# Two layers of a hybrid diffusion backbone on one core: the borders between blocks worked in two sets of 320 tokens

## The reference

```
h = rmsnorm(x, g[2*s]) * (1 + scale[s]) + shift[s]
y = block_s(h)          # s=0: FFN, s=1: token mixing, s=2: FFN
x = x + (0.5 or 1) * gate[s] * rmsnorm(y, g[2*s+1])
FFN(h) = (silu(h @ w1) * (h @ w3)) @ w2      # 1024 -> 2816 -> 1024
```

## Time and profile before

| | us |
|---|---|
| median of 3 runs | 3273.2 |
| the profiled execution, its own time | 3275.5 |
| its span, first to last instruction | 3273.7 |
| PE busy | 2971.1 (91%) |
| POOL busy | 1361.0 (42%) |
| DVE busy | 972.3 (30%) |
| ACT busy | 580.3 (18%) |
| mean granted PE clock | 0.951 |

### The profile page before, as it was taken

How to read it: one execution, slowest core, us unless ns; L and a number is a source line. 1 busy time by engine, 2 the same in 40 slices (tenths; PEclk the granted TensorE clock), 3 DMA queues, 4 the chain that set the end, 5 groups by cost and what they waited for, 6 DMA issues and landing times.

```text
span 3273.7 us, 50932 instructions
## 1 busy us (share of the span) xinstructions
PE 2971.1 (91%) x21012; PEld 2812.1 (86%) x21012; DVE 972.3 (30%) x1580; ACT 580.3 (18%) x974; POOL 1361.0 (42%) x1556
## 2 busy tenths in 40 slices
PE   6999999898978899999979999997988787999996
PEld 3999999798877799999969999997988776999996
DVE  3110111624546531011141101116245465210112
ACT  2000001312213421000130000013131145110111
POOL 1445445333322335544524454453332223455553
PEclk8999999899888899999989999998998888999998
DMA  6332332211102112233213323322110021112211
GB/s 261 129 124 88 129 128 89 86 67 44 44 26 90 53 42 67 83 129 128 96 65 128 116 96 129 124 92 84 51 52 30 27 91 52 62 62 89 70 64 59
DMA packets 46370, 281.89 MB, mean 86 GB/s; under 512 B 5089, under 2 KB 10721, under 8 KB 20513
## 3 DMA queue, kind: packets, MB, share of 16 engines
q1 hardware_dynamic: 39024, 259.46, 22.2%
q10 hardware_dynamic: 7216, 20.60, 1.7%
HBM read 270.07 MB, written 9.97 MB: 86 GB/s over the span
## 4 chain that ended last, share of the span: by engine, by line
PE 84%; DVE 8%; ACT 3%; issue 2%; DMA 1%; DVEq 1%; POOL 0%; ACTq 0%; SPq 0%
PE ps L527 25%; PE ps L529 24%; PE ps L528 24%; PE ps L559 2%; ACT rstd L964 2%; PE ps L753 1%; PE ps L696 1%; ACT arena L964 1%; DVE rstd L1386 1%; PE ps L716 1%; PE ps L736 1%; DMA first_raw<-in_w_mod 1%; DVE arena L1350 1%; PE ps L548 1%; PE ps L760 1%
## 5 line engine op out<-in xcount | busy, mean ns | idle before, releaser
L477 POOL TENSOR_SCALAR wsplit<-raw 128x512 fp32r<-128x512 f32 (+2 forms) x776 | 443.6, 600 | 1872.3 <-issue 831.2
L527 PE MATMUL ps<-h,wsplit 128*128 128x320 f32 (+1 forms) x3488 | 1106.1, 317 | 76.6 <-DVE rstd L1386 32.4
L528 PE MATMUL ps<-h,wsplit 128*128 128x320 f32 (+1 forms) x3488 | 1086.4, 311 | 0.0
L529 PE MATMUL ps<-h,wsplit 128*128 128x320 f32 (+1 forms) x3488 | 1086.0, 311 | 0.0
L482 POOL TENSOR_TENSOR wsplit<-raw,wsplit 128x512 fp32r<-128x512 f32 (+2 forms) x776 | 924.4, 1224 | 0.0
L527 PEld LDWEIGHTS ps<-h,wsplit 128*128 128x128 f32 (+1 forms) x3488 | 662.1, 190 | 116.2 <-DVE rstd L1386 57.6
L528 PEld LDWEIGHTS ps<-h,wsplit 128*128 128x128 f32 (+1 forms) x3488 | 663.0, 190 | 0.0
L529 PEld LDWEIGHTS ps<-h,wsplit 128*128 128x128 f32 (+1 forms) x3488 | 661.8, 190 | 0.0
L527 PE MATMUL ps<-hidden,wsplit 128*128 128x320 f32 x1408 | 435.8, 310 | 3.6 <-issue 3.6
L529 PE MATMUL ps<-hidden,wsplit 128*128 128x320 f32 x1408 | 435.1, 309 | 0.0
L528 PE MATMUL ps<-hidden,wsplit 128*128 128x320 f32 x1408 | 435.1, 309 | 0.0
(11 more groups left out here) (171 smaller groups left out, 2517.0 us busy)
## 6 DMA issues: line engine op xcount, KB each, us to landing
raw<-in_w SPq DMA_DIRECT2D x88, 1024.0 KB, 6.4
raw<-in_w_mod SPq DMA_DIRECT2D x60, 1024.0 KB, 4.9
raw<-in_w SPq DMA_DIRECT2D x64, 704.0 KB, 4.2
raw<-in_w_in SPq DMA_DIRECT2D x30, 1024.0 KB, 4.9
first_raw<-in_w_mod SPq DMA_DIRECT2D x12, 1024.0 KB, 5.0
raw<-in_w_out SPq DMA_DIRECT2D x8, 768.0 KB, 4.3
spill<-xT ACTq DMA_DIRECT2D x2, 2560.0 KB, 7.6
xT<-spill ACTq DMA_DIRECT2D x2, 2560.0 KB, 13.8
```

The costliest lines, as they stand in the source:

```text
L477: nc.gpsimd.tensor_scalar(w[:, 0, at], src[:, at], 1.0, 1.0, ALU.mult, ALU.mult)\
L527: mm(out, w[0], x[0], start=first, stop=False)
L528: mm(out, w[0], x[1], start=False, stop=False)
L529: return mm(out, w[1], x[0], start=False, stop=last)
```

## The change

- The last two down units of an FFN (units 6 and 7 of the second group) are claimed together and worked as half 0 of both, then half 1 of both; the sum of squares of half 0 is multiplied within half 1 of the first. DVE evacuates them by halves.
- The output projection makes 16 pieces of six matmuls, first half 0 of all 8 tiles, then half 1, in a ring of six PSUM banks.
- All squares, roots, outgoing and incoming norm steps of a border are made for tokens 0 to 319 and then for 320 to 639 (`tokens`, `token_parts`), with DVE's outgoing steps of half 1 placed between its incoming steps of half 0, and ACT's squares likewise.
- The first products of a block (`enter`) run for half 0 as its h comes, with the sums of half 1's squares in between, then for half 1. In border 0 two pieces of the input projection (half 0) stand between the two halves of the gates. In border 1 the first **two** up units are worked together. In border 2 it is the first up unit.
- Counters' initial increments for layer 1 are made at the head of the whole program of PE and DVE.
- The output is two transfers, each when its half of x is there, issued by SP in the main block.
- The four modulation operations for the next borders (`prepare`) stand between the outgoing steps of half 1.

```diff
-for _u, _parts in ((U_C, FEAT), (U_C + 1, FEAT), (U_C + 2, TOK), (U_C + 3, TOK),
+for _u, _parts in ((U_C, FEAT_BY_HALF), (U_C + 1, FEAT), (U_C + 2, TOK), (U_C + 3, TOK),
...
+                for a in range(2):
+                    sp.wait_ge(signals[-1].x_ready, x_count(2, a, KT - 1))
+                    sp.dma_start(O["y"][:, :, tokens(a)], xT[:, :, tokens(a)]).then_inc(y_out, 16)
+                sp.wait_ge(y_out, 32)
...
+                    def border_sums(b, l_in, s):
+                        for k in range(4):
+                            x_sums(l_in, s, 0, k)
+                        y_sums(b, 1)
+                        for k in range(4, KT):
+                            x_sums(l_in, s, 0, k)
+                    def enter(s, units, more=None):
+                        for a in range(2):
+                            pe.wait_ge(sig.rstd_ready, in_count(l, s, a))
                             for k in range(KT):
+                                pe.wait_ge(sig.h_ready, h_count(l, s, a, k))
+                                for base, blocks in units:
+                                    for b, w in enumerate(blocks):
+                                        c = base + (2 * b + a) * BANK
+                                        last = three_pass(ps[0:w.shape[3], c:c + HALF], (w[:, 0, k, :], w[:, 1, k, :]),
+                                                          [h2[:, p, k, tokens(a)] for p in range(2)],
+                                                          k == 0, k == KT - 1)
+                                    if a and k == KT - 1:
+                                        last.then_inc(sig.unit_done, 1)
+                                if a == 0:
+                                    x_sums(l, s, 1, k)
+                            if a == 0 and more:
+                                more()
...
+                            elif mods:
+                                enter(s, [(claim(f), up_weights(f))])
+                                turn()
                             else:
+                                enter(s, [(claim(u), up_weights(u)) for u in (f, f + 1)])
...
+                        bases = [claim(n + KT - 2 + u) for u in range(2)]
+                        for a in range(2):
+                            for u in range(2):
+                                w = split_ap(l, n + KT - 2 + u, GF_T * P).rearrange("p s (f c) -> p s f c", f=GF_T)
+                                c = bases[u] + a * BANK
+                                for k in range(GF_T):
+                                    last = three_pass(ps[:, c:c + HALF], (w[:, 0, k, :], w[:, 1, k, :]),
+                                                      [a2[:, p, k, tokens(a)] for p in range(2)],
+                                                      k == 0, k == GF_T - 1)
+                                    if a and u == 0 and k == 7:
+                                        y_sums(s, 0)
+                                last.then_inc(sig.unit_done if a else half_done, 1)
...
-                        first_products(1, base, (w,))
+                        enter(1, [(base, (w,))], lambda: dense(2))
...
-                    sums(1, U_GATES)
-                    sums(2, U_GATES)
+                    border_sums(0, l, 1)
                     gates()
-                    dense(11)
+                    dense(9)
...
+                    ring = (0, 1, 4, 5, 6, 7)
+                    for a in range(2):
+                        for m in range(KT):
+                            q = a * KT + m
+                            if q >= len(ring):
+                                pe.wait_ge(sig.y_sum, q - len(ring) + 1)
...
+                            if q == KT + 4:
+                                y_sums(1, 0)
+                    border_sums(1, l, 2)
                     ffn(2, 1)
-                    sums(5, U_ALL[l])
+                    if l + 1 < DEPTH:
+                        pe.wait_ge(sig.unit_evac, EV(U_ALL[l] - 1))
+                        mod(U_FFN[0], l=l + 1, sig=signals[l + 1])
+                        border_sums(2, l + 1, 0)
+                    else:
+                        y_sums(2, 1)
...
+                            half_y(0, 0)
+                            add_square(b, KT - 3)
+                            half_y(1, 0)
+                            add_square(b, KT - 2)
+                            add_square(b, KT - 1)
+                            half_y(0, 1)
+                            for k in range(3):
+                                out_step(b, 0, k)
+                            add_square(b, KT)
+                            half_y(1, 1)
+                            for k in range(3, 5):
+                                out_step(b, 0, k)
+                            add_square(b, KT + 1)
+                            for k in range(5, KT + 1):
+                                out_step(b, 0, k)
+                        for k in range(3):
+                            out_step(b, 1, k)
+                        if prepare:
+                            dve.drain()
+                            prepare()
                         for k in range(KT + 1):
+                            if l_in < DEPTH:
+                                in_step(l_in, s, 0, k)
+                            if k + 3 <= KT:
+                                out_step(b, 1, k + 3)
+                        if l_in < DEPTH:
+                            for k in range(KT + 1):
+                                in_step(l_in, s, 1, k)
```

More of the change, by code:

```diff
@@ L88 @@
 FEAT = [("feat", m, a) for m in range(2) for a in range(2)]
+FEAT_BY_HALF = [("feat", m, a) for a in range(2) for m in range(2)]
 TOK = [("tok", 0, 2), ("tok", 2, 2), ("tok", 4, 1)]
@@ L549, in mod_turn, with first_sums @@
                         last.then_inc(sig.mtr_done, 1)
[L551 to L555, removed]
-                            for k in range(KT):
[L557 to L568, removed]
+                    def first_sums():
+                        pe.wait_ge(sig.acc_add, KT)
+                        for a in range(2):
+                            last = mm(ps[:, (2 + a) * BANK:(2 + a) * BANK + HALF], ones, rstd[:, tokens(a)],
+                                      start=True, stop=True)
+                        last.then_inc(sig.ss_done, 1)
@@ new lines, in y_sums, with x_sums @@
+                    def y_sums(b, a):
+                        y = Y_STEPS[b]
+                        pe.wait_ge(sig.acc_add, KT + Y_BASE[b] + y.index((KT - 1, a)) + 1)
+                        mm(ps[:, (2 + a) * BANK:(2 + a) * BANK + HALF], ones, rstd[:, tokens(a)],
+                           start=True, stop=True).then_inc(sig.ss_done, 1)
+                    def x_sums(l, s, a, k):
+                        pe.wait_ge(xsq_ready, xsq_count(l, s, a, k))
+                        last = mm(ps[:, (2 + a) * BANK:(2 + a) * BANK + HALF], ones, yT[:, k, tokens(a)],
+                                  start=k == 0, stop=k == KT - 1)
+                        if k == KT - 1:
+                            last.then_inc(signals[l].ss_done, 1)
@@ new lines, in h_upper, with border @@
+                    def h_upper(l, s, a, k):
+                        act.wait_ge(signals[l].hmul_ready, h_count(l, s, a, k))
+                        for c, cols in token_parts(a):
+                            last = fn(h2[:, 0, k, cols], yT[:, k, cols], ACT.Identity,
+                                      bias=modS[:, 3 * KT * s + k, c:c + 1])
+                        last.then_inc(signals[l].h_hi, 1)
+                    def border(b, l_in, s):
+                        out = lambda a: root(l, rstd_count(l, b, f"out{a}"), a)
+                        last = l_in == DEPTH
+                        if b == 1:
+                            for i in range(KT + 5):
+                                y_step(b, i)
+                            out(0)
+                            for i in range(KT + 5, 2 * KT):
+                                y_step(b, i)
+                        else:
+                            for i in range(KT):
+                                y_step(b, i)
+                                if i == KT - 3:
+                                    ln_exp()
+                            out(0)
+                            y_step(b, KT)
+                            if not last:
+                                x_square(b, 0, 0)
+                                x_square(b, 0, 1)
+                            y_step(b, KT + 1)
+                        if last:
+                            out(1)
+                            return
+                        for k in range(2 if b != 1 else 0, 6):
+                            x_square(b, 0, k)
+                        out(1)
+                        for k in (6, 7):
+                            x_square(b, 0, k)
+                        root(l_in, in_count(l_in, s, 0), 0)
+                        for k in range(KT):
+                            h_upper(l_in, s, 0, k)
+                            x_square(b, 1, k)
```

(3 more changed lines are left out.)

294 lines of the change are left out of this document (163 added, 131 removed).

## The result

The changed kernel takes **3327.0 us** (median of 4 runs, 3326.3 to 3329.4) against 3273.7 for the kernel before beside it; the ratio is 1.0165, 95% interval 1.0153 to 1.0178. Forecast were 3322, and 3293 to 3346 as the range. The profiled execution took 3329.4, with a span of 3327.6 (before 3273.7) at a mean granted clock of 0.950 (before 0.951); it is the slowest of the four.

The account below looks back on a forecast made before the run. TensorE (PE), 84% of the span, was taken as the bound, losing by waits and half clock. Border 0 twice 20.8, border 1 twice 27.0, border 2 1.0 and the end -0.3 gave +48.5 us: 3322, range 3293 to 3346.

Parts of the forecast that it names:

- F: Border 2 between the layers: 45.4 us against 53.3, increments' wait gone, with the paired down units' cost +1.0 us.
- G: Kernel end: 17.7 us behind unit 7, plus 8.9 for the paired down units, against 26.9: -0.3 us.
- A: Last down units at each FFN end, four times: PE waits 6.3 us for unit 7's split, restarts slow: +8.9 us.
- B: Border 0, twice, from unit 7's end to the gates' end: 40.9 us against 41.4, -0.5 us.
- C: Dense pieces between the gate halves, twice: PE stands 7.0 us waiting for ACT, no gain, cold restart: +2.0 us.
- D: Border 1, twice: half-sum delays PE, two up units leave little room, 62.2 us against 59.9: +4.2 us.
- E: Third up unit, twice: two units hold both buffers, PE waits 7.3 us for POOL's split, restarts cold: +9.3 us.
- The contention: Border 0: POOL's split of the first input unit slows twelve DVE operations, +5.7 us, bounds 0 and 7.6.
- the half-sum behind piece 12: Border 1, output projection: PE waits for eight ACT steps; with the sum itself +1.9 us.
- the second transfer: Kernel end: output transfer of 1280 KB, in no row, taken as 5.6 us, between half and all of 7.9.
- The price of a half add: DVE's half adds in the borders: taken as 0.40 us, between 0.37 and 0.48.
- The rival that the overlap wins: Splits in place in time at FFN ends and third up unit: -3 us, 3250 without contention; chance 0.10.

Follow-up runs that it names:

- e4: Changed kernel with both dense pieces of the input projection behind both halves of the gates again: 3320.8 us, ratio 1.0141 to the kernel before.
- e1: Changed kernel with unit 7 claimed only behind half 0 of unit 6: 3297.4 us, ratio 1.0069 to the kernel before.
- e8: Changed kernel with the last two down units in turn, each claimed by itself, half-sum in half 1 of unit 7: 3301.2 us, ratio 1.0084.
- e2: Changed kernel with half 1 of the first two up units in border 1 worked one unit after the other: 3311.3 us, ratio 1.0111.
- e6: Changed kernel with POOL's split of the first input unit cut to 8 columns an instruction, leaving out part of the computation: 3314.8 us, ratio 1.0125.
- e5: Changed kernel with unit 7 claimed late, one up unit entering border 1, and dense pieces behind the gates: 3272.5 us, ratio 0.9994.
- e7: Kernel before with only layer 1's initial increments moved to the head of PE's and DVE's programs: 3265.5 us, ratio 0.9977.

## Why the prediction was right, point by point

Measured in the profiled execution, layer 0 (F and G where they are):

| step | forecast | measured | from |
|---|---|---|---|
| A, x4 | +8.9 | +9.2 | unit 5's end to unit 7's end 28.6 (571.4 to 600.0), before 19.4 |
| B, x2 | -0.5 | +0.3 | unit 7's end to the gates' end 41.7 (to 641.7) for 41.4 |
| C, x2 | +2.0 | +3.0 | 14.5 shift at 1126.82, less A, B and 2.0 at the start; e4: 3.05 |
| D, x2 | +4.2 | +2.3 | second up unit 1205.8 |
| E, x2 | +9.3 | +9.4 | 23.5 from second to third up unit, before 14.1 |
| F | +1.0 | +2.1 | shift from 26.3 to 28.4 |
| G, with its A | -0.3 | +0.2 | 17.7 behind unit 7, before 26.9 |

With A inside F and G, 2 x (9.2 + 0.3 + 3.0) + 2 x (2.3 + 9.4) + 2.1 + 0.2 = 50.7. The spans differ by 53.9. Another 2.0 is there before the first up unit (86.3 for 84.3): the first weights arrive at 19.9 in place of 16.7. That is no effect of the change, as e1 and e8, with the same code there, have them at 17.2 and 17.0. Of the last 1.2 most is in border 1 of layer 1, where the kernel before is 0.9 faster than in layer 0 (89.9 for 90.8): its restart before the output projection costs 1.6 there and 2.5 in layer 0, behind the same wait of 3.9 (last section).

That the sum came so near is in part luck: D was 1.9 too high, twice, while A, B, C and F, all too low, make up for it.

**A and E, the two that decide**, held in cause and size: waits of 6.4 and 7.3 for the 6.3 and 7.3, slow products for 4.4 to 5.4 us for the 4.5 (a choice between bounds, no reading: behind the stop at 1112.30 the kernel before has 5.5), and e1 and e2 took them away by the buffer alone. Together they are 4 x 9.2 + 2 x 9.4 = 55.6 us; all the rest, C included, is -4.9.

**B.** The chain without contention came out as worked (adds 0.40 apart, roots as priced), and so did its end: 41.7 for 40.9. The contention was 6.1 by e6, for 5.7. The Trainium skill's page SBUF — State Buffer (section "SBUF: two separate sides") has a DVE operation with two SBUF inputs and one of POOL take the shared pair for a whole instruction; the 7.6 which that gave is 1.5 too much, and my 5.7 was 0.4 too little. The rows agree with taking turns (POOL's four take 5.91 where nearly alone they take 5.02, and DVE's start as far apart as POOL's), but POOL's 1.3 and DVE's 0.40 would make 1.7 a turn, and it is 1.47, so some of each overlaps.

**C** was undersized by 1.0. The place was right (6.87 of wait on ACT, by its own order of work). The slow stretch behind it lasts from 648.7 to 654.2, 20 products, which costs 2.6 and not 2.0; the last 0.4 isn't traced.

**D** failed in one term: the half-sum behind piece 12 cost 0.85, not 1.9. PE's wait for it was 0.15; the projection starts at the slow clock, which gives the chain of squares time, and that I had left out (argued, not tested). The parts of the rest are off in both directions (last product to half 0's root 19.5 for 21.2, half 0 of both units 21.3 for 20.0) and leave 61.3 for 62.2.

**F**: 46.2 behind unit 7 for 45.4; how much of it the contention makes (8.1 in the forecast) no run separates. **G**: 17.7 for 17.7; the second transfer takes 5.7 from its issue (3321.9) to the end, for the 5.6 taken between the bounds.

**The price of a half add**, 0.40, was what the chains of B, F and G lay on, and it is 0.40 (3312.37, 3312.77 and on, in the end). The Trainium skill's page VectorE: DVE Perf Modes (section "The TRN2 errata") gives 0.49 for it; that is what the trace has as its duration (0.48), while its successor starts 0.40 later. Halving doubles only what doesn't overlap, 0.07 us an add.

**The rival that the overlap wins** was right that the two waits decide between a loss and none: with the splits nearly in place the change is as fast as before (e5). The 3250 for no contention as well was not run; by e6's difference it would be some 12 us under e5, 3260, and lower by what the contention in F costs.

## What to carry to other kernels

Before two units are worked side by side to let the next stage begin early, count the buffers of whatever prepares their operands: with two buffers, pairing two units stops the preparation of the third, and the stop (6.4 and 7.3 us here) costs more than the overlap wins. Claim late and release early: order the work so that one buffer is asked for only behind the first half of the other, and is done with before the other's last half begins. And look at waits on bookkeeping first: increments at a program's head gave some 8 us for no work at all. Then change the end before the borders inside: the end of the kernel, with nothing behind it to collide with, is where working in halves paid (7 us), while inside, with the waits nearly gone, it won nothing in border 0 and lost in borders 1 and 2 (e5). An outcome of zero for the whole can hide this, so take the trace apart by stretches.

## What the runs showed of the hardware

- POOL's upper parts (one input) hold DVE up too: half adds start 0.81 apart beside them (602.06 to 603.69) and POOL's four take 3.06 in place of 2.4. In e7, beside adds of 640 columns, it is POOL alone that pays: its four take 4.54, while DVE's adds keep their 0.735. What decides who waits stays open.
- POOL's instructions on 8 columns still take 0.36 and 0.42 each (1.46 and 1.67 for four), for 0.59 and 1.26 on 512 columns (2.37 and 5.02 for four).
- What a stop of PE costs by the clock, over its waits for POOL in the traces of all eleven kernels: behind waits of 0.8 to 2.2 us no product but the first was slow; behind those of 3.9 us 19 to 23 products were slow (2.4 to 2.9 us more) in 21 of 22 cases; behind those of 6.4 us 11 to 22 (1.4 to 2.8); behind those of 7.3 us 16 (2.1); behind the one of 6.9 us in the kernel after 20 (2.6). From 3.9 us on a longer stop did not cost more, and the same stop did not always cost the same.
- The 22nd case is the kernel before in layer 1: some 1.1 us at full clock, then 13 slow products, which cost 1.6 us. The same place in layer 0, then in layer 1 (columns as in the earlier trace rows):

```profile
1112.30:1117.30 5.00, 5.00 (x19) 5.00 (x20) 0.82 (x1) 0.51 (x1) 3.51 (x3) 0.50 0.20 28
2734.54:2739.54 5.00, 5.00 (x24) 5.00 (x25) 0.82 (x1) 1.12 (x3) 3.52 (x3) 0.66 0.20 28
```
